# Hybrid GLA and sparse-attention layer: key and query stacks interleaved with the gate projection, its last pieces bank by bank, compressed heads transposed in pairs

## The reference, cut to what matters

```python
proj = rms_norm(h) @ w_in        # GLA part, and n_q, k/v of 3 branches, gates n_g, n_z
# per block of 128 queries:
p_cmp = softmax(q . kc)          # 63 compressed blocks
o_cmp = p_cmp @ vc
p_slc = softmax(q . k_slc)       # n_sel = 16 of 16 blocks: causal attention over all keys
p_win = softmax(q . k_win)       # window of 512
o = g[..., 0:1] * o_cmp + g[..., 1:2] * o_slc + g[..., 2:3] * o_win
o_nsa = o * silu(n_z)
mixed = concat([o_gla, o_nsa]) @ w_out   # then norm, residual and the per-layer input
```

## Time and profile before

| | us |
|---|---|
| median of 3 runs | 883.62 (883.04 to 884.14) |
| the profiled execution | 882.08, of which the span is 880.3 |
| PE busy | 836.7 (95%) |
| DVE busy | 541.5 (62%) |
| ACT busy | 461.3 (52%) |
| POOL busy | 375.6 (43%) |

### The profile page before, as it was taken

One profiled execution on the slowest core, in us unless ns is written; L12 is line 12 of the kernel. 1 busy time (PEld: TensorE's weight loads), 2 busy tenths in 40 slices (PEclk: granted clock), 3 DMA queues, 4 the chain that ended last, 5 costly groups with the idle time before them and its releaser, 6 DMA issues.

```text
span 880.3 us, 12437 instructions
## 1 busy us (share of the span) xinstructions
PE 836.7 (95%) x4638; PEld 688.7 (78%) x4638; DVE 541.5 (62%) x937; ACT 461.3 (52%) x930; POOL 375.6 (43%) x331
## 2 busy tenths in 40 slices
PE   8999999999999999998889999999989999999996
PEld 7878788888888788777667777777757888887884
DVE  2770459852735406777899997899965035373445
ACT  4513144134122026676889988889866252625424
POOL 3312018153321121673457655356534455463554
PEclk9999899999999999999999999999999999999998
DMA  9501011111011111310000000000008623232337
GB/s 310 119 13 49 24 45 48 38 37 48 26 48 36 35 50 48 94 37 1 1 0 1 1 1 2 0 1 1 1 1 290 220 88 97 77 102 73 97 99 247
DMA packets 38158, 55.19 MB, mean 63 GB/s; under 512 B 11073, under 2 KB 17489, under 8 KB 38098
## 3 DMA queue, kind: packets, MB, share of 16 engines
q1 hardware_dynamic: 37810, 53.34, 19.8%
q0 software_dynamic: 288, 1.05, 0.7%
HBM read 49.13 MB, written 5.25 MB: 62 GB/s over the span
## 4 chain that ended last, share of the span: by engine, by line
PE 75%; DVE 12%; ACT 8%; issue 3%; POOL 1%; DMA 0%; DVEq 0%; SPq 0%; ACTq 0%; POOLq 0%
PE psum L884 45%; PE psum L1147 3%; DVE pT_lo L2090 3%; PE psum L1164 3%; PE psum L996 3%; ACT pT_hi L1489 3%; PE psum L1165 2%; PE psum L1131 2%; ACT p_win L1475 2%; PE psum L910 2%; PE psum L1132 2%; DVE p_slc L2064 1%; PE psum L805 1%; PE psum L807 1%; PE psum L806 1%
## 5 line engine op out<-in xcount | busy, mean ns | idle before, releaser
L1610 POOL TENSOR_TENSOR w_lo<-w_raw,w_hi 128x512 fp32r<-128x512 f32 x126 | 180.1, 1433 | 343.8 <-ACT w_hi L1270 343.4
L1270 ACT ACTIVATE w_hi<-w_raw 128x512 fp32r<-128x512 f32 x126 | 79.4, 635 | 310.4 <-PE psum L884 300.2
L2090 DVE TENSOR_TENSOR pT_lo<-psum,pT_hi 128x512 fp32r<-128x512 f32 (+1 forms) x148 | 100.1, 685 | 17.9 <-ACT pT_hi L1489 16.8
L1489 ACT ACTIVATE pT_hi<-psum 128x512 fp32r<-128x512 f32 (+1 forms) x148 | 86.8, 593 | 32.3 <-PE psum L1147 31.3
L884 PE MATMUL psum<-w_hi,xT_hi 128*128 128x512 f32 x256 | 101.1, 395 | 1.7 <-DVE gla_state_b L1971 1.7
L884 PE MATMUL psum<-w_lo,xT_hi 128*128 128x512 f32 x256 | 99.7, 389 | 0.0
L884 PE MATMUL psum<-w_hi,xT_lo 128*128 128x512 f32 x256 | 99.7, 389 | 0.0
L1164 PE MATMUL psum<-pT_hi,v_hi_lo 128*128 128x512 f32 x132 | 60.8, 461 | 18.1 <-DVE pT_lo L2090 17.5
L1131 PE MATMUL psum<-kT_hi_hi,qT_hi_lo 128*128 128x384 f32 (+3 forms) x192 | 70.5, 371 | 4.5 <-DVE neg_max L2064 4.1
L1666 POOL TENSOR_SCALAR p_slc<-p_slc,gate_over_sum 128x512 f32<-128x512 f32 (+7 forms) x40 | 64.5, 1624 | 1.8
L1475 ACT ACTIVATE p_slc<-p_slc,neg_max 128x512 f32<-128x512 f32 (+7 forms) x80 | 58.0, 727 | 5.1 <-DVE neg_max L2064 4.9
(11 more groups left out here) (280 smaller groups left out, 1979.0 us busy)
## 6 DMA issues: line engine op xcount, KB each, us to landing
w_raw<-in_w_in SPq DMA_DIRECT2D x56, 256.0 KB, 2.7
w_raw<-in_w_out SPq DMA_DIRECT2D x32, 256.0 KB, 2.6
w_raw<-in_ple_gate SPq DMA_DIRECT2D x32, 256.0 KB, 2.5
x_tok<-in_x SPq DMA_DIRECT2D x8, 512.0 KB, 6.5
h_tok<-in_x SPq DMA_DIRECT2D x8, 512.0 KB, 5.5
out<-h_tok SPq DMA_DIRECT2D x6, 512.0 KB, 5.5
w_raw<-in_ple_proj SPq DMA_DIRECT2D x8, 256.0 KB, 2.6
cmp_w<-in_cmp_w_k SPq DMA_DIRECT2D x16, 64.0 KB, 2.2
```

What stands on the lines that cost most here:

```text
L1270: act.activation(w_hi(i)[:, 0:w], w_in(i)[:, 0:w], ACT.Copy).then_inc(s_whi, 1)
L1489: act.activation(PTh[0:n, u % 4], bank(4 + u % TRING)[0:n], ACT.Copy).then_inc(s_phi, 1)
L1610: pool.tensor_tensor(w_lo(i)[:, 0:w], w_in(i)[:, 0:w], w_hi(i)[:, 0:w].bitcast(F32), ALU.subtract).then_inc(s_wlo, 1)
L2090: dve.tensor_tensor(PTl[0:n, u % 4], bank(4 + u % TRING)[0:n], PTh[0:n, u % 4].bitcast(F32), ALU.subtract).then_inc(s_plo, 1)
```

## The change

Four things are changed.

1. **Stacks.** Four of the eight second-half stacks (q 0, k 0, q 1, k 2) go between the gate pieces, as soon as the gate pieces that read the memory beneath them are done (1, 1, 3, 3), in banks 5 and 4. To make this possible the hi and lo keys become one tensor `kT` whose slot for a head covers the memory of two pieces. The other four (q 2, k 1, q 3, k 3) are given step number 16 in the scheduler, and spread over the units of the first steps.
2. **Gate end.** Pieces 0 to 4 are run whole as before; pieces 5, 6 and 7 are run bank by bank (`gate_end(b)`, 9 matmuls each), and the banks' order is 6, 7, 1, 3. Scores are put between them. The four sigmoids are planned as one operation. The first two turns may stand before the gate's end (they only wait for the first 13 stacks); their pT_hi waits until the last weight piece is split, for the fourth unit until the last bank, and their pT_lo until the last bank is done.
3. **Compressed units.** Two heads are transposed at once: 2 transposes of 128 x 128 instead of 4 of 128 x 63, so that the tile is 128 x 256 instead of 63 x 512. The values are then 4 matmuls of 256 columns against two zero-padded copies of the compressed values (one on partitions 0 to 62, one on 64 to 126) instead of 2 of 512. All heads' columns are in the order 0, 2, 1, 3.
4. **What this needs.** At the start DVE clears the compressed values (128 x 512); in the compression 2 more 63 x 64 products, 1 more copy on ACT and 1 more subtraction on DVE; one small clearing of the pads of p_cmp.

```diff
+    VC = sm("vc_hi_lo", [P, NKV, 2, P], F32R)
+    KT = sb("kT", [P, 4, 2, SEQ], F32R, R1 + 32768)
-        + [(kind, h, 1) for hs in ((0, 1), (2, 3)) for kind in "qk" for h in (hs if kind == "q" else (hs[0] // 2, hs[0] // 2 + 2))]
-    first_half = 9
-    stack_bank = [4, 5, 0, 2, 4, 5, 4, 5, 4] + [1, 3] * 4
-    gate_bank = {"nzA": (1, 3, 0, 2), "nzB": (1, 3, 6, 7)}
+        + [("q", 0, 1), ("k", 0, 1), ("q", 1, 1), ("k", 2, 1), ("q", 2, 1), ("k", 1, 1), ("q", 3, 1), ("k", 3, 1)]
+    first_half, soon = 9, 13
+    stack_bank = [4, 5, 0, 2, 4, 5, 4, 5, 4] + [5, 4, 5, 4] + [1, 3, 1, 3]
+    stack_piece = {9: 1, 10: 1, 11: 3, 12: 3}
+    gate_bank = {"nzA": (1, 3, 0, 2), "nzB": (6, 7, 1, 3)}
+    WHOLE = 5
...
+        def gate_end(b):
+            c = cidx["nzB"]
+            out, cols = bank(gate_bank["nzB"][b]), slice(b * P, (b + 1) * P)
+            for k in range(WHOLE, KD):
+                i = piece0[c] + k
+                if b == 0:
+                    pe.wait_ge(s_wlo, i + 1)
+                wh, wl = Wh[:, i % SPLIT], Wl[:, i % SPLIT]
+                pe.matmul(out, wh[:, cols], XTh[:, k, 512:1024], start=False, stop=False)
                 pe.matmul(out, wh[:, cols], XTl[:, k, 512:1024], start=False, stop=False)
                 mm = pe.matmul(out, wl[:, cols], XTh[:, k, 512:1024], start=False, stop=(k == KD - 1))
...
+            if br == 0:
+                for a in range(2):
+                    mm = pe.transpose(out[:, a * P:(a + 1) * P],
+                                      probs(s)[:, 2 * a:2 * a + 2].rearrange("p g j -> p (g j)"), ident)
...
+            if br == 0:
+                for par in range(2):
+                    cols = slice(256 * par, 256 * par + 256)
+                    pe.matmul(out[:, cols], VC[:, kv, par], PTh[:, u % 4, 0:256], start=(par == 0), stop=False)
+                    mm = pe.matmul(out[:, cols], VC[:, kv, par], PTl[:, u % 4, 0:256], start=False, stop=False)
...
         def tile_hi(u):
-            act.activation(PTh[0:n, u % 4], bank(4 + u % TRING)[0:n], ACT.Copy).then_inc(s_phi, 1)
+            elif u < 3:
+                act.wait_ge(s_wlo, piece0[cidx["nzB"] + 1])
+            else:
+                act.wait_ge(s_bank, bank0[cidx["nzB"] + 1])
+            act.activation(PTh[:, u % 4, 0:w], bank(4 + u % TRING)[:, 0:w], ACT.Copy).then_inc(s_phi, 1)
...
         def tile_lo(u):
+            if u < 4:
+                dve.wait_ge(s_bank, bank0[cidx["nzB"] + 1])
```

More of the change, by code:

```diff
@@ L930, in compressed @@
                                    W2[:, n], start=True, stop=True)
+            for kv in range(NKV):
+                mm = pe.matmul(bank(5)[64:64 + NCMP, kv * DH:(kv + 1) * DH], HCT[:, 1, kv * 64:kv * 64 + NCMP],
+                               W2[:, 1], start=True, stop=True)
             mm.then_inc(s_cout, 1)
@@ L1143, in turn @@
             else:
-                pe.wait_ge(s_qlo, first_half)
-            n = min(P, span(qt, br)[1])
-            for g in range(GRP):
-                mm = pe.transpose(bank(4 + u % TRING)[0:n, g * P:(g + 1) * P],
-                                  probs(s)[:, g, i * P:i * P + n], ident)
+                pe.wait_ge(s_qlo, soon)
+            out = bank(4 + u % TRING)
+            if br == 0:
[3 more added lines that the diff above has]
+            else:
+                for g in range(GRP):
+                    at = head_column(g)
+                    mm = pe.transpose(out[:, at:at + P], probs(s)[:, g, i * P:i * P + P], ident)
             mm.then_inc(s_pt, 1)
@@ L1437, in _ @@
         act.wait_ge(s_cout, 1)
-        act.activation(VC[0:NCMP, :, 0:DH], bank(5)[0:NCMP, 0:P].rearrange("p (c d) -> p c d", c=2),
-                       ACT.Copy).then_inc(s_cvh, 1)
+        act.wait_ge(s_vcz, 1)
+        for par in range(2):
+            r = slice(64 * par, 64 * par + NCMP)
+            ins = act.activation(VC[r, :, par, 0:DH], bank(5)[r, 0:P].rearrange("p (c d) -> p c d", c=2), ACT.Copy)
+        ins.then_inc(s_cvh, 1)
         split_chunk("gv", {4: [lambda: decay_exponents(0)], 5: [lambda: decay_exponents(1)],
@@ L1517, in _ @@
             elif kind == "gate_sig":
-                gate_sigmoid(1, n)
+                for b in range(4):
+                    gate_sigmoid(1, b)
             elif kind == "stack_hi":
```

124 lines of the change are left out of this document (77 added, 47 removed).

## The result

The changed kernel takes 873.63 us (872.95 to 873.77) beside 883.37 us for the kernel before: a ratio of 0.9887, interval 0.9875 to 0.9898, or 10.0 us. A second measurement beside another set of runs gave 0.9892. The forecast was 6.05 us.

A forecast was written before the change was run, and what follows sets the result against it. PE alone bounds the gate stretch, DVE and ACT 404 to 431 us, and nobody has slack afterwards. Head -3.35, compressed units -3.1, additions +0.4 give -6.05 us: 883.62 to 877.6 us, by itself 874.5 to 880.5, range 873.5 to 882.0.

The forecast's parts named there:

- The rest of the order: From about the 100th operation, order the same to swaps of neighbours: no effect forecast, 1 us either way in the range.
- Head, 3.35 us: Moved stacks and gate's end, up to output 0: 4.85 us earlier, less 2.0 for late stacks, plus 0.5.
- PE's clock should not fall: After the gate's end: no PE gap reaches 3.24 us, so clock 1.00 from 404 to 431 us; otherwise 1.5 us come back.
- Compressed units, 3.1 us less 0.4: 14 units at 0.22 us each, engine savings weighted by chain shares, 3.1 us faster; additions cost 0.4.
- The additions, 0.4 us: Two more compression products on PE, 0.3 us, and pads, 0.1 us; extra copy, subtraction and clearing hidden.
- 1.6 us less: Sign in the timeline: from output 0 to the last unit, 3.1 - 1.5 = 1.6 us less than before.
- The lock of DVE and GpSimd: Gate multiplications beside GpSimd's work: by the skill's rule up to 1.2 us for DVE; the row was kept, nothing taken.
- The late start: First tile_lo 4.45 us later and not made up, slower: 887.0 us, or 885 with half of it; chance 0.09.
- the head brings nothing: After the gate's end DVE or ACT hold one another; only compressed units gain: 880.9 us; chance 0.17.
- compressed units hide: Shorter compressed units bring nothing, only the head's 3.35 us counts: 880.7 us; chance 0.08.
- More than the sum: Ring limits almost everywhere (4.8 instead of 3.1 us) and head gains 4.85 us: 874.4 us; chance 0.14.
- the ring's prices: Serial turn, high, low chain shared by two banks: half an engine's given-back work times 14, 1.5, 1.4, 1.9 us slower.

The follow-up runs named there:

- plan_measured: Changed kernel's instructions, scheduler's durations for a compressed unit set to those its trace shows (200, 380, 410 ns for 220, 420, 420); 877.57 us, ratio 0.9942.
- head_alone: Changed kernel with the compressed units as before and the scheduler's old durations for them; new stacks and gate end stay; 880.32 us, ratio 0.9963.
- head_units_old_plan: Changed kernel with all its instructions, but the scheduler's old durations for compressed units (430, 600, 720 ns); 877.25 us, ratio 0.9927.
- the old plan: Scheduler's old durations for a compressed unit (430, 600, 720 ns for turn, high, low), here with all the changed kernel's instructions; 877.25 us, ratio 0.9927.
- units_alone_old_plan: Kernel before in exactly its order, with only the compressed units in pairs; 879.49 us, ratio 0.9960.
- plan_middle: Changed kernel's instructions, scheduler's durations for a compressed unit half-way to the old ones (325, 510, 570 ns); 876.04 us, ratio 0.9924.
- the filler: Changed kernel in the order of the old durations, plus twelve 512-column matmuls into an unread bank to fill two PE gaps; 876.5 us, ratio 0.9928.

## Why the prediction was wrong

The direction, the places and the sizes of the two large terms in the old order were right. The time, 873.63 us, came 0.9 us under the 874.5 to 880.5 in which the forecast was to hold by itself, at the lower edge of the wider range that began at 873.5: one effect was put at nothing.

- **The failed step: "The rest of the order (from about the 100th operation) is the same to swaps of neighbours: none forecast, 1 us either way in the range."** What the runs show in its place: the three durations that were edited with the units are worth 3.5 us by the order alone (0.9927 to 0.9887, the same instructions), -2.1 us in the kernel before, and five orders of the same instructions span 0.0055, 4.9 us. With 3.3 for the head and 3.1 for the units, 3.5 for the order makes up the measured 10.0 but for rounding. Nor are the swaps of neighbours only: in the kernel before the durations move 103 of 417 operations of DVE, in the changed one some of DVE's by up to ten places. From these runs the bound should have been some 3 us either way, and 877.6 would then have been a fair middle: the mean of the five orders is 876.1. That the order actually written fell on the good side was luck: no reason was given for it, and the durations of the trace gave the worst of the five (plan_measured).
- **Head, 3.35 us: right as a sum, and its places in the new order.** It measures 3.3 alone. The gate's last matmul begins at 409.55 (forecast 408 to 410), the first tile_lo at 410.05 (409.1), the gate multiplications end at 415.1 (414.5 was the limit set; their first waits behind a compressed sum), output 0 begins at 427.01 (426 to 427). From 383 us to the gate's end PE has one gap of 0.37 us, none over 0.5. The clock is 1.00 from 404 to 431. "PE's clock should not fall" does not hold in the order of the old durations: head_alone and head_units_old_plan, with the same head, have 3.4 us at half clock and reach output 0 1.7 to 2.5 us later.
- **Compressed units, 3.1 us less 0.4: right in the old order (3.5 and, with the new head, 6.4 - 3.3 = 3.1), too small in the new one (6.0).** The durations were as forecast: 416 ns (415), 380 ns (0.4 us), half the transposes. The weights by the chain's shares were not: TensorE, ScalarE and VectorE got 52, 26 and 22% of their savings, and returned 28, 41 and 81% in the dense stretch of the new order. In the old order only the sum was measured, so that it came out right may be luck. The shares of a chain say where it passed, not what an engine's shortening gives.
- **The additions, 0.4 us:** the gate's first matmul starts at 370.0 instead of 369.8 us. That is less than such starts differ between traces, so it bears the forecast out only as small.
- **From output 0 to the last unit "1.6 us less":** it was 4.1 us (229.4 to 225.3), and 2.2 us in the old plan (429.63 to 656.81).
- **The lock of DVE and GpSimd:** here the prediction misread its row. It said that DVE lost nothing that shows in 2.80 us for four multiplications; alone the four take 2.48 us (head_alone), and one of those in the kernel before took 0.99 us instead of 0.68. In the changed kernel a 128x252 product of GpSimd lies beside them. It takes 1.03 us instead of 0.67, and one multiplication takes 1.16 us instead of 0.68: the 2.96 us of the four. In head_alone the same product took 2.85 us, ending 0.5 us after the last of the four, and DVE lost nothing:

```profile
412.34 1.03 POOL L1707 TENSOR_TENSOR p_cmp<-p_cmp,masks 128x252 f32<-128x252 f32 x1 [2.32 <-DVE p_cmp L2120]
```

```profile
412.96 2.85 POOL L1679 TENSOR_TENSOR p_cmp<-p_cmp,masks 128x252 f32<-128x252 f32 x1 [2.57 <-DVE p_cmp L2085]
```

```profile
412.80 2.48 DVE L2045 TENSOR_TENSOR nsa_zT<-nsa_zT,sigmoid_tmp 128x512 f32<-128x512 f32 x4
```

The Trainium skill (SBUF — State Buffer, "Who interferes with whom") lets whoever comes second wait for the whole operation. These traces agree: GpSimd's product runs from 412.34 to 413.38 us, and the multiplication that was issued in that time ends at 413.93, 0.55 us behind it. The price for DVE was 0.48 us, where the prediction, in keeping to its row, took none and named 1.2 us as the most.

- **Rivals.** The late start and "the head brings nothing" fall by output 0 and by head_alone; "compressed units hide" by units_alone_old_plan. "More than the sum" comes nearest (874.4), for another reason: of the ring's prices (1.5, 1.4 and 1.9 us for TensorE, ScalarE and VectorE) the dense stretch bears out the second (1.2), has half of the first (0.8) and one and a half times the third (3.0), and the head gave no 4.85.

Not settled: whether the kernel before's own order was a poor or an average one. Of its instructions three orders were run, at 0.9976, 1 and 1.0024. Nor is it known what in an order makes it good.

## What to carry to other kernels

Where a scheduler's durations are edited together with the code, the order is a second change: measure it apart, by the old durations with the new code, and give the forecast a spread that comes from a few neighbouring orders. If 10 ns in the plan move the time by about 1 us, then choosing among orders is a tuning of its own (here 3 us for no instruction). To tell such orders apart, compare the distance between two landmarks inside the traces: in two pairs of traces of one order it repeated to less than a tenth of a us here, where whole runs of one kernel differed by 1 us and more. An engine's saving should be priced by giving that engine its old work back, not by its share of the chain or its busy time: in the dense stretch PE and DVE were both busy 90%, and returned three and eight tenths.

## What was not expected of the hardware

A small difference decided whether the clock fell. In the traces with the changed head, PE's gaps between 414 and 421 us come to 3.4 us in head_alone, head_units_old_plan and plan_middle, and all three then have 3.4 us at half clock (from 422.3, 420.6 and 420.4 us on). In the eleven others without the filler they come to 2.6 to 3.0 us, and none has a dip there; the changed kernel's two gaps of 1.42 and 1.56 us are among them. Whether it is this sum that counts or how the gaps lie, no run tells.

A 128x256 tile costs ACT 380 ns and DVE 416 where 128x512 costs 593 and 686: by a straight line through the two, an estimate, a fixed part of about 167 ns (2 x 380 - 593) and 146 ns (2 x 416 - 686), so that halving a tile saves only some 0.2 to 0.27 us.
